# One opening stage, modulation products moved beside other stages, constant tables loaded where they are used

## The reference

```
sc = silu(c); sc_ctx = silu(c_ctx)            # (1024,)
mx = split(sc @ mod_w[i] + mod_b[i], 6)       # mod_w[i]: 1024 x 6144
mc = split(sc_ctx @ mod_w[i] + mod_b[i], 6)
hx = rms_norm(x, norm_g[i, 0]) * (1 + mx[1]) + mx[0]
x  = x + mx[2] * mixer(hx, hc)
x  = x + mx[5] * swiglu(modulated(rms_norm(x, norm_g[i, 1]), mx[3], mx[4]))
```

## Time and profile before

| | us |
|---|---|
| median of 3 runs | 5654.5 |
| profiled execution, its own time | 5663.57 |
| its span, first to last instruction | 5661.9 |
| TensorE busy | 4529.2 (80%) |
| TensorE weight load busy | 3749.6 (66%) |
| VectorE busy | 2533.3 (45%) |
| ScalarE busy | 1469.0 (26%) |
| GpSimd busy | 564.8 (10%) |

### The profile page before, as it was taken

One profiled execution on the slowest core, in us unless ns is written; L12 is line 12 of the kernel. 1 busy time (PEld: TensorE's weight loads), 2 busy tenths in 40 slices (PEclk: granted clock), 3 DMA queues, 4 the chain that ended last, 5 costly groups with the idle time before them and its releaser, 6 DMA issues. The chain is left out here.

```text
span 5661.9 us, 87284 instructions
## 1 busy us (share of the span) xinstructions
PE 4529.2 (80%) x35259; PEld 3749.6 (66%) x35259; DVE 2533.3 (45%) x3619; ACT 1469.0 (26%) x2457; POOL 564.8 (10%) x743
## 2 busy tenths in 40 slices
PE   6738879999975388765996939469999994766998
PEld 1614568888852287763995838358888893444997
DVE  1354533335444644444444232344335854765444
ACT  0224522113243211102222221222113332323322
POOL 0101110001111111211001000010001112320000
PEclk9859989999996599986998965589999996768999
DMA  5254622222363312233331322222222343342332
GB/s 203 79 179 144 206 85 60 65 65 65 117 214 126 105 51 59 57 119 106 94 95 57 110 77 59 81 85 62 60 64 64 104 123 109 122 153 82 97 94 71
DMA packets 671281, 561.56 MB, mean 99 GB/s; under 512 B 113480, under 2 KB 582208, under 8 KB 670952
## 3 DMA queue, kind: packets, MB, share of 16 engines
q1 hardware_dynamic: 640680, 453.94, 26.7%
q0 software_dynamic: 30272, 102.84, 4.9%
HBM read 459.97 MB, written 96.71 MB: 98 GB/s over the span
## 5 line engine op out<-in xcount | busy, mean ns | idle before, releaser
L86 PE MATMUL acc<-h_hi,w_hi 128*128 128x258 f32 (+2 forms) x4416 | 1403.1, 318 | 47.9 <-DVE h_lo L455 41.3
L88 PE MATMUL acc<-h_hi,w_lo 128*128 128x258 f32 (+2 forms) x4416 | 1399.0, 317 | 0.0
L87 PE MATMUL acc<-h_lo,w_hi 128*128 128x258 f32 (+2 forms) x4416 | 1396.7, 316 | 0.0
L86 PEld LDWEIGHTS acc<-h_hi,w_hi 128*128 128x128 f32 x4416 | 833.2, 189 | 115.3 <-issue 24.5
L87 PEld LDWEIGHTS acc<-h_lo,w_hi 128*128 128x128 f32 x4416 | 834.5, 189 | 60.5 <-issue 0.5
L88 PEld LDWEIGHTS acc<-h_hi,w_lo 128*128 128x128 f32 x4416 | 833.3, 189 | 59.0
L334 ACT CAST w_hi<-staged 128x1024 fp32r<-128x1024 f32 (+1 forms) x414 | 406.9, 1028 | 646.4 <-PE acc L88 390.1
L442 DVE TENSOR_TENSOR w_lo<-staged,w_hi 128x1024 fp32r<-128x1024 f32 (+1 forms) x414 | 480.4, 1200 | 142.5 <-ACT w_hi L334 139.5
L86 PE MATMUL acc<-hidden_hi,w_hi 128*128 128x512 f32 (+1 forms) x1200 | 419.5, 350 | 64.2 <-DVE hidden_lo L573 64.2
L483 DVE COPY offset<-acc 128x2 f32<-128x2 f32 x276 | 43.7, 158 | 927.7 <-PE acc L88 925.1
L87 PE MATMUL acc<-hidden_lo,w_hi 128*128 128x512 f32 (+1 forms) x1200 | 419.1, 349 | 0.0
(11 more groups left out here) (428 smaller groups left out, 6882.2 us busy)
## 6 DMA issues: line engine op xcount, KB each, us to landing
wmod<-in_mod_w SPq DMA_DIRECT2D x16, 3072.0 KB, 13.0
staged<-in_w_ffn_in SPq DMA_DIRECT2D x88, 512.0 KB, 5.0
staged<-in_ffn_w_in SPq DMA_DIRECT2D x88, 512.0 KB, 5.0
w<-in_w_mod SPq DMA_DIRECT2D x12, 2048.0 KB, 8.2
wmod<-in_w_mod SPq DMA_DIRECT2D x8, 3072.0 KB, 10.7
rows<-acum SPq DMA_DIRECT2D x48, 512.0 KB, 3.8
staged<-in_ssd_w_in SPq DMA_DIRECT2D x42, 512.0 KB, 4.9
proj<-gate POOLq DMA_DIRECT2D x40, 384.0 KB, 2.6
```

What stands on the lines that cost most here:

```text
L86: nc.tensor.matmul(out, w[0], x[0], start=start, stop=False)
L87: nc.tensor.matmul(out, w[0], x[1], start=False, stop=False)
L88: return nc.tensor.matmul(out, w[1], x[0], start=False, stop=stop)
```

## The change

The opening stages (tables, vectors of both blocks, first modulation, tokens) become one stage `opening`. It loads the small vectors as six packed tiles, computes only columns 0 to 2047 of the first modulation, with the weights as the stationary operand (128 x 128) and the 2 conditioning vectors as the moving one, so that the result is already in columns and nothing is stored, and turns the tokens between the products:

```
+    n_mod = 2 * KD * P // NC                       # 4
+            AFTER = ((0, 1), (2, 3), (4, 5), ())
+            @block.sync
+                sp.dma_start(ident[:], tables[0][1])...
+                for r, n, src in packs[0][1]:
+                    sp.dma_start(vectors[0][r:r + n, :], src)...
+                for s in range(n_mod):
+                    sp.dma_start(wbuf[s][:], wr[:, :, s * NC:(s + 1) * NC])...
+                    for i in AFTER[s]:
+                        sp.dma_start(rows[i][:], tokens[i][0])...
+            @block.tensor
+                def modulate(s):
+                    pe.wait_ge(S[f"w_loaded{s}"], 16)
+                    for j in range(NC // P):
+                        for k in range(KD):
+                            mm = nc.tensor.matmul(sums[:, s * (NC // P) + j, :], wbuf[s][:, k, j * P:(j + 1) * P],
+                                                  conds[0][:, k, 0:2], start=(k == 0), stop=(k == KD - 1))
+                for s in range(n_mod):
+                    if s == n_mod - 1:
+                        for v in range(1, len(packs)):
+                            turn_vectors(v)
+                    modulate(s)
+                    for i in AFTER[s]:
+                        turn_tokens(i)
+            @block.gpsimd      # 24 small loads: the other five packs and the two matrices of ones
+            @block.vector
+                for b in range(2):
+                    nc.vector.tensor_tensor(modT[:, 0:2 * KD, b], sums[:, :, b], b_cols[:, 0:2 * KD], ALU.add)
```

The remaining 4096 columns of that modulation go beside the attention over all keys (512 columns a head instead of 768), the first block's second modulation beside the window attention, the second block's first beside the neighbourhood attention, and its second into `rwkv_features`, two pieces of 768 columns to a tile:

```
-    attention(..., near=a["neighbour_bias"], beside=second[2][1][0:3])
+    attention(..., near=a["neighbour_bias"], beside=products_of(second[0], 0))
 def rwkv_features, load of tile m (SyncE):
+                    if first and s == 0:
+                        sp.dma_start(reset[:], reset_src).then_inc(reset_loaded, 16)
+                    for j in range(2):
+                        if not (type(m) is int and m == 0):
+                            sp.wait_ge(mod_ready, 2 * m + (j - 1))
+                        sp.dma_start(wbuf[j][:], w_mod[:, :, bass.ds(m * (2 * MN) + j * MN, MN)])...
 TensorE, between the gate product and the bonus product:
+                    for j in range(2):
+                        modulate(m, j)
 VectorE, between bonus_in and the copy of the gate:
+                    for j in range(2):
+                        dve.wait_ge(mod_ready, 2 * m + (j + 1))
+                        ...
+                        nc.vector.tensor_copy(mod_row[j][:], mod_ps[j][:]).then_inc(mod_copied, 1)
 GpSimd, after the stores of bonus and gate: 2 x 4 stores of the rows
```

```
-                load_tables(nc, [(cos, ...), (sin, ...), (edge, ...), (sinks, ...)])
-                columns(nc, ident, [(gains, a["qk_gains"])])
+    rope(nc, proj, rot, 0, 5, consts, gains, tables=(cos, sin))
 def rwkv_chunks:
+                sp.dma_start(masks[:], masks_src).then_inc(S["masks_loaded"], 16)
                 steps_of(sp, NCH, load)
-        modulation_rows(nc, *first[2][0][0:3])
-        load_tokens(nc, xT, ident, [(a["ctx"][0], 0), (a["x"][0], CTX)])
-        modT = columns_of(mods[0])
+        opening(nc, [...], ident, packs, (cond, cond_2), tokens, xT, a["w_mod"][0], b_first, first[0][4])
-            columns(nc, ident, [(mu, a["shift_mu"][0])])
-            next_modT = columns_of(mods[1])
+        columns_of((first[0], 2 * KD), (first[1], 0))
```

More of the change, by code:

```diff
@@ L677, in _, with opening @@
                         nc.vector.tensor_copy(xT[:, 4 * g:4 * g + 4, c:c + P], turned[n % 4][:]).then_inc(turned_used, 1)
[L680 to L711, removed]
+def opening(nc, tables, ident, packs, conds, tokens, xT, w, b_cols, modT):
     NC = 512
-    steps = 6 * D // NC
+    n_mod = 2 * KD * P // NC
     wr = w.rearrange("(k p) n -> p k n", p=P)
@@ L717, in modulation_rows @@
         sb, ps = memory(nc, ctx)
[L718 to L731, removed]
+        wbuf = [sb(f"w{s}", [P, KD, NC]) for s in range(n_mod)]
@@ L733, in _ @@
+        with stage(nc, *names) as (block, *sems):
+            S = dict(zip(names, sems))
+            AFTER = ((0, 1), (2, 3), (4, 5), ())
             @block.sync
             def _(sp):
[L735 to L739, removed]
+                sp.dma_start(ident[:], tables[0][1]).then_inc(S["ident_loaded"], 16)
+                for r, n, src in packs[0][1]:
+                    sp.dma_start(vectors[0][r:r + n, :], src).then_inc(S["vec_loaded0"], 16)
+                for s in range(n_mod):
+                    sp.dma_start(wbuf[s][:], wr[:, :, s * NC:(s + 1) * NC]).then_inc(S[f"w_loaded{s}"], 16)
+                    for i in AFTER[s]:
+                        sp.dma_start(rows[i][:], tokens[i][0]).then_inc(S[f"rows_loaded{i}"], 16)
+                sp.wait_ge(S["tables_loaded"], 16 * (len(tables) - 1))
@@ L741, in _, with turn_vectors @@
             @block.tensor
             def _(pe):
[L743 to L750, removed]
+                def turn_vectors(v):
+                    n = packs[v][2]
+                    pe.wait_ge(S[f"vec_loaded{v}"], 16 * len(packs[v][1]))
+                    if v >= 2:
+                        pe.wait_ge(S["vec_used"], v - 1)
+                    nc.tensor.transpose(small[v % 2][:, 0:n], vectors[v][0:n, :], ident[0:n, 0:n]).then_inc(S["vec_turned"], 1)
@@ L753, in _ @@
             def _(dve):
[L754 to L768, removed]
@@ L771, in modulation_columns, with keep @@
-def modulation_columns(nc, ident, rows, b_cols, modT):
-    with ExitStack() as ctx:
-        sb, _ = memory(nc, ctx)
-        cols = [sb(f"cols{b}", [P, 6 * KD]) for b in range(2)]
-        columns(nc, ident, [(cols[b], rows[b]) for b in range(2)])
-        with stage(nc, "added") as (block, added):
+                def keep(v):
+                    n = packs[v][2]
+                    dve.wait_ge(S["vec_turned"], v + 1)
+                    nc.vector.tensor_copy(packs[v][0][:, 0:n], small[v % 2][:, 0:n]).then_inc(S["vec_used"], 1)
@@ new lines, in _ @@
+                keep(0)
+                for s in range(n_mod):
+                    if s == n_mod - 1:
+                        for v in range(1, len(packs)):
+                            keep(v)
+                    for i in AFTER[s]:
+                        for g in range(2):
+                            n, c = 2 * i + g, tokens[i][1]
+                            dve.wait_ge(S["turned_ready"], n + 1)
+                            nc.vector.tensor_copy(xT[:, 4 * g:4 * g + 4, c:c + P], turned[n % 4][:]).then_inc(S["turned_used"], 1)
@@ L876, in _ @@
             def _(sp):
+                for table, origin in tables:
+                    sp.dma_start(table[:], origin).then_inc(tables_loaded, 16)
                 def load(i, s, first):
@@ L989, with attention @@
 TILES_NEAR = [whole_tile(i, True) for i in range(LAT // P)]
-def attention(nc, ident, heads, qk, q_row, k_row, per_kv, v, v_row, mix, mix_row, tiles, edge=None, sinks=None, near=None, beside=None):
+def attention(nc, ident, heads, qk, q_row, k_row, per_kv, v, v_row, mix, mix_row, tiles, edge=None, sinks=None, near=None, beside=None, tables=()):
     QT = len(tiles)
@@ L1245, in _ @@
                 split_q(0)
+                if tables:
+                    dve.wait_ge(tables_loaded, 16 * len(tables))
                 top(0)
@@ L1378, with rwkv_features @@
 NCH = TOK // CH
-def rwkv_features(nc, mixed, w2, a2, g2, cols, block_ones, reset, arrays, dec, bonus, gate):
+def rwkv_features(nc, mixed, w2, a2, g2, cols, block_ones, reset_table, arrays, dec, bonus, gate, beside):
+    reset, reset_src = reset_table
     (kk_c, ka_c, rk_c, w0_c, a0_c) = cols
@@ new lines, in ssd_layer @@
+            ssd_readout(nc, ident, ones, ssd_ys, proj, ssd_gain, wide)
+        cond, first = conditions(a["w_mod"], b_first, "first")
+        cond_2, second = conditions(a["mod_w_2"], b_second, "second")
+        norms = lambda t, i: t[:, KD * i:KD * (i + 1)]
+        tokens = [(src[t:t + P, :], c0 + t) for src, c0 in ((a["ctx"][0], 0), (a["x"][0], CTX)) for t in range(0, src.shape[0], P)]
+        opening(nc, [(ident, a["identity"]), (ones, a["all_ones"]), (block_ones, a["block_ones"])], ident, packs, (cond, cond_2), tokens,
+                xT, a["w_mod"][0], b_first, first[0][4])
```

313 lines of the change are left out of this document (196 added, 117 removed).

## The result

| | before | after |
|---|---|---|
| median, us | 5655.34 (4 runs, 5653.19 to 5657.86) | 5561.77 (4 runs, 5554.53 to 5565.43) |
| ratio after / before, 95% interval | | 0.9833 [0.9816, 0.985] |
| profiled execution, its own time and span, us | 5663.57, 5661.9 | 5565.43, 5563.8 |

What follows compares the result with a forecast made beforehand. TensorE was taken to bound the opening's products, and six gaps of 54.5 us to lie on the path; terms summed to -107.7 us, from 5663.6 to 5556 profiled, 5547 as median, own range 5532 to 5562, 8-in-10 range 5510 to 5574.

Steps and rivals of the forecast that it cites:

- Opening: Opening merged into one stage: ends at 78 us instead of 148.5, weight products at the half clock, -70.5 us.
- Rival 1: Opening products get the full clock after the first tile: opening ends at 54, kernel takes 5523 us; chance 0.22.
- The argument from the earlier trace: In gla_chunks TensorE was busy 60.0 of 60 us at clock 0.50, so the opening was taken at the half clock.
- Gaps, columns, tables: Small-load gaps of 7.2 to 11.6 us lie wholly on the path; column stages change and tables precede stages' first loads.
- the taps' 10.9 us: Before the last between nothing remains of the columns stage: -10.9 us.
- Attention over all keys: Each head's product has 128 columns a group instead of 192: -5.5 us, between nothing and 7.5 us gained.
- Products in `rwkv_features`: Added modulation products, 2 x 4.64 us per tile, run behind the gate product and stay hidden with 9 us to spare.
- the stall: In rwkv_features stores land late beside weight loads, at half the bandwidth: 2 us in three of four tiles, +6.0 us.
- rival 2: rwkv_features stores wait for all weights in flight (+18 us), tables cost 2 us more each (+12): 5577 us; chance 0.08.
- Last stores: GpSimd's 8 small stores follow the last store of rwkv_features' last tile, 0.52 us each: +4.2 us.
- +0.9 for the masks: Masks loaded ahead of rwkv_chunks' first loads cost one issue and part of 0.66 MB: +0.9 us.
- Rival 3: Products in rwkv_features are not covered, weights and products lie on the path: +123 us, 5670 us; chance 0.02.

Runs made afterwards that it cites:

- Late loads: Changed kernel, with rwkv_features' next modulation weights loaded only after the current tile's first-direction stores have landed: 5535.0 us, ratio 0.979, stage 198.4 us.

## Why the prediction was right, and where not

- **Opening, right.** The end at 76.9 for 78, by the reasoning given: half clock, 64 loads in 13.7 us for 14.0, DMA ahead. That it is this close is in part luck: the turns took 3.3 to 3.7 us a pair of row tiles for 2.7 and the first product began 1.2 us late, and the second tile's 10.9 us made up for it; in executions without that the opening ended at 80.6. Rival 1 failed as a forecast, but its price was right: with 128 columns the opening ended at 53.5 us, for its 54. The argument from the earlier trace rows (busy without a pause and still at 0.50) decided, and the runs bear it out: with TensorE equally busy, two or 32 columns streamed behind each load left the clock at its half and 128 raised it. The Trainium skill, page "TensorE: Matmul & The Clock Gate", section "LDWEIGHTS (loading the stationary operand)", gives 107 ns for a load of 128 columns, from which 6.8 us a tile is an estimate: the trace comes near it at the full clock (7.31, with 128 columns streamed) and has twice that at the half (13.7).
- **Gaps, columns, tables, right.** The gaps of the earlier trace rows, read as wholly on the path, came off as read, the taps' 10.9 us to the tenth; where a table went ahead of a stage's loads, the difference to the forecast is 0.1 to 1.6 us (`rope`, SSD, GLA).
- **Attention over all keys: the term mis-sized.** -5.5 was taken between 0 and -7.5; it measured -9.6. The product followed its columns: 2.81 to 1.95, and 4.64 to 2.65 at the half clock, so 7 x 0.86 + 1.99 = 8.0 us. Over the ten profiled executions that have this stage as changed it took 170.6 us on average, over three of the kernel before 178.4: -7.7, so about 2 of the 9.6 are spread. What failed was the hedge between the two ends, where the row spoke for the upper.
- **Products in `rwkv_features`, right that they are hidden; the stall mis-sized.** The collision was seen at its place and in its order: weights issued just before the stores. It was priced at 2 us a tile, and the waits show 5.3 in each of three; the tiles got 4.4, 5.4 and 2.8 us longer (12.6 for 6.0), the third with part of it won back by a higher clock. Failed: "at half the bandwidth for itself". The landing of the smallest store, the last of five, is the one waited for, and beside the weights it went from 4.0 to 10.3 us. Late loads took the stall away whole (the three tiles got 5.3, 5.3 and 5.2 us shorter), so that nothing else is in it, and the rule of the Trainium skill's page "DMA: Bandwidth & Descriptors", section "Issuing engines are not separate DMA queues", holds: loads of SyncE delayed stores of GpSimd. This is rival 2's mechanism at about half of its price: 15.9 us of waits, where the forecast had 6 and rival 2 24.
- **Last stores: the term mis-sized, a cost not seen.** +4.2 was forecast, +5.5 measured, made of 2.9 us of stores behind the tail and 2.6 us of drain for 32 more DMAs (32 x 0.082). The prediction priced a GpSimd DMA only by its issue.
- **`rwkv_chunks`: open in part.** +0.9 for the masks against 1.6 us at the first product. Of the rest of +10.4, some 5 us are how the two profiled executions lay about their means; some 4 us may be real, and no run shows a cause.
- **Rival 3** was refuted by the timeline: the products began when the gate product ended, without a wait for weights.

The 14.1 us between forecast and gain are then: `rwkv_features` +7.6 (stall +6.6, its end +1.3), `rwkv_chunks` +9.5, attention -4.1, the rest of the ledger -3.4, and 4.5 because the profiled execution lay 8.2 us above the median before but only 3.7 after.

## What to carry to other kernels

Bulk loads moved beside a stage cost nothing on its idle engines and yet delay its stores (here the small one from 4.0 to 10.3 us): find the store whose landing a buffer waits for, and issue the loads behind it, not ahead. Where TensorE's work is nearly all weight loading, pad the moving operand until the clock is granted; here 128 columns halved the time of a product that needs two, and turns ahead of the products did the same for two tiles with 64. Where a stage's end waits for GpSimd, count the DMAs that it issued there, since each added 0.082 us before the barrier in this kernel, and let SyncE issue small ones where it has nothing behind them.

## What the hardware did that I had not expected

- GpSimd's drain at the end of a stage: 0.082 us for each DMA it has issued since the last (5: 0.46; 16: 1.37; 40: 3.31; 48: 3.97; 80: 6.59 us), for stores of 1.5 to 384 KB, and though all had landed.
- The granted clock with TensorE busy without a pause: 0.50 with 2 columns streamed a load but for some 3 us after turns, no better with 32; with 64 it stayed at 1.00 where turns had raised it and stayed at 0.50 elsewhere (one execution); 1.00 in most of the opening with 128.
- The listed clock reads 1.00 until the first record of the clock in a trace, whatever the pace. In the two executions with the longest openings the first record comes only at 109 us or later, and the products ran at 48 to 49 per 10 us, the half clock's pace, under a listed 1.00. In the kernel before the records begin at 36.6 us, so the 1.00 of the earlier trace rows holds from there; the products before it took 0.8 us each for 0.42 after. The pace of a known instruction is the surer reading.
- One stage of 11136 small products took from 517.8 to 530.7 us in eight executions of kernels that are the same in it.
